# Norm 1 of layer 0 made tile by tile inside the last five vectors of the modulation stage

## The reference, cut to what matters

```python
shift1, scale1, gate1, shift2, scale2, gate2 = jnp.split(mod, 6, axis=-1)   # mod = silu(c) @ w_mod[l] + b_mod[l]
h = rms_norm(x, lp["g_norm1"]) * (1 + scale1) + shift1
u = h @ lp["w_in"]          # the first dense product of the layer; four attention mixers read it
...
x = x + gate1 * mixed
h = rms_norm(x, lp["g_norm2"]) * (1 + scale2) + shift2
x = x + gate2 * expert_choice_ffn(h, ...)
```

## Time and profile before

| | |
|---|---|
| median of 3 runs | 2919.36 us |
| profiled execution, its own time | 2924.13 us |
| its span, first to last instruction | 2922.1 us |
| TensorE busy | 2708.1 us, 93% |
| VectorE, ScalarE, GpSimd busy | 66%, 53%, 16% |
| mean granted clock of TensorE | 0.972 |

### The profile page before, as it was taken

How to read it: one execution, slowest core, us unless ns; L and a number is a source line. 1 busy time by engine, 2 the same in 40 slices (tenths; PEclk the granted TensorE clock), 3 DMA queues, 4 the chain that set the end, 5 groups by cost and what they waited for, 6 DMA issues and landing times.

```text
span 2922.1 us, 40619 instructions
## 1 busy us (share of the span) xinstructions
PE 2708.1 (93%) x13616; PEld 1916.2 (66%) x13616; DVE 1929.7 (66%) x3006; ACT 1555.4 (53%) x2270; POOL 465.5 (16%) x359
## 2 busy tenths in 40 slices
PE   7799999999998999999989999998999699999994
PEld 1387777777773666666658777787777366666662
DVE  7653466435256999999955346653525799999994
ACT  6534443334223877777743444333422387777773
POOL 1030001212211112222113000031122112111111
PEclk9799999999998999999999999999999899999997
DMA  9621111212346999999982111121234599999994
GB/s 362 235 78 42 33 37 49 68 37 68 120 158 223 375 381 376 378 380 378 384 281 77 43 33 37 41 76 37 65 120 151 189 371 385 374 379 380 380 382 165
DMA packets 191183, 593.74 MB, mean 203 GB/s; under 512 B 23628, under 2 KB 33674, under 8 KB 191054
## 3 DMA queue, kind: packets, MB, share of 16 engines
q1 hardware_dynamic: 171646, 527.68, 48.9%
q0 software_dynamic: 19408, 64.37, 7.4%
HBM read 566.73 MB, written 25.23 MB: 203 GB/s over the span
## 4 chain that ended last, share of the span: by engine, by line
PE 79%; DVE 8%; issue 5%; ACT 4%; DMA 3%; SPq 0%; POOL 0%; ACTq 0%; DVEq 0%; POOLq 0%
PE bank L499 22%; PE bank L501 20%; PE bank L500 20%; PE bank L920 4%; PE bank L892 4%; PE bank L910 2%; ACT high L1123 2%; DVE low L1446 2%; DMA ring<-in_w_mod 1%; PE bank L683 1%; DVE st L1692 1%; DVE att L1527 1%; PE bank L1074 1%; PE bank L1035 1%; DVE sigr L1622 1%
## 5 line engine op out<-in xcount | busy, mean ns | idle before, releaser
L1123 ACT ACTIVATE high<-ring 128x1024 fp32r<-128x1024 f32 (+1 forms) x976 | 1023.0, 1052 | 412.3 <-PE bank L501 370.0
L1833 DVE TENSOR_TENSOR low<-ring,high 128x1024 fp32r<-128x1024 f32 x736 | 880.1, 1220 | 73.3 <-ACT high L1123 71.5
L499 PE MATMUL bank<-high,hT_high 128*128 128x512 f32 (+2 forms) x1280 | 521.2, 407 | 25.3 <-ACT sigr L1202 13.6
L500 PE MATMUL bank<-low,hT_high 128*128 128x512 f32 (+2 forms) x1280 | 486.5, 380 | 0.0
L501 PE MATMUL bank<-high,hT_low 128*128 128x512 f32 (+2 forms) x1280 | 484.8, 379 | 0.0
L499 PE MATMUL bank<-high,xeT_high 128*80 128x512 f32 x1056 | 418.8, 397 | 5.8 <-issue 3.5
L501 PE MATMUL bank<-high,xeT_low 128*80 128x512 f32 x1056 | 416.5, 394 | 0.0
L500 PE MATMUL bank<-low,xeT_high 128*80 128x512 f32 x1056 | 416.2, 394 | 0.0
L1446 DVE TENSOR_TENSOR low<-ring,high 128x1024 fp32r<-128x1024 f32 (+2 forms) x240 | 285.5, 1208 | 131.1 <-ACT high L1123 130.0
L1307 ACT ACTIVATE att<-bank,st 128x640 f32<-128x640 f32 (+3 forms) x200 | 136.7, 684 | 348.8 <-DVE st L1697 254.2
L499 PEld LDWEIGHTS bank<-high,hT_high 128*128 128x128 f32 x1280 | 243.9, 191 | 79.1 <-ACT sigr L1202 18.2
(11 more groups left out here) (253 smaller groups left out, 3288.2 us busy)
## 6 DMA issues: line engine op xcount, KB each, us to landing
ring<-in_w_e_gate SPq DMA_DIRECT2D x256, 512.0 KB, 6.2
ring<-in_w_e_up SPq DMA_DIRECT2D x256, 512.0 KB, 7.0
ring<-in_w_e_down SPq DMA_DIRECT2D x256, 512.0 KB, 6.6
ring<-in_w_mod SPq DMA_DIRECT2D x64, 512.0 KB, 6.9
ring<-in_w_gate SPq DMA_DIRECT2D x64, 512.0 KB, 4.6
ring<-in_w_in SPq DMA_DIRECT2D x24, 512.0 KB, 3.8
U<-in_w_mod SPq DMA_DIRECT2D x20, 512.0 KB, 5.0
ring<-in_w_branch SPq DMA_DIRECT2D x16, 512.0 KB, 5.5
```

The source lines that it names most:

```text
L499: nc.tensor.matmul(out, lhs[0], rhs_high, start=start, stop=False)
L500: nc.tensor.matmul(out, lhs[0], rhs_low, start=False, stop=False)
L1123: A(high[:, HSLOT[g], :, 0:w], ring[:, SLOT[g], :, 0:w], ACT.Copy).then_inc(high_done, 1)
L1833: V.tensor_tensor(low[:, SLOT[ahead], :, :], ring[:, SLOT[ahead], :, :], high[:, HSLOT[ahead], :, :].bitcast(F32), ALU.subtract).then_inc( ...
```

## The change

The five tiles of norm 1 of layer 0 are made inside the stage, tile m within vector m+3:

- ScalarE squares tile m behind the first split of vector m+3's step, and writes the high part of the turned tile behind the last split, ahead of `mod_evac`.
- VectorE scales and shifts tile m behind the fifth split of the same step, and writes its low part ahead of the next step's first split.
- TensorE turns tile m behind the last chunk of the vector, into banks 4 to 7. Those banks held the results of `mod_tail`; that result now goes into banks 0 to 3, over the vector's own partial sums.
- `mod_tail(q-1)` stands behind the second chunk of vector q in place of the last, and `mod_copy(q-1)` behind the third split of step q in place of the second split of step q+1. GpSimd loads shift 1 and scale 1 after the store of vector 1, before after that of vector 2.
- TensorE waits for all of norm 1 before the first dense product, whose five tiles then follow with no turns between them. The wait for the last `mod_copy` moves from the end of the stage to the turning of the compressed keys.

Layer 1 is as before.

```diff
+NORM_FROM = N_FIRST - T
+        def norm_bank(q, m, half):
+            return (2 * (m % 2) + half) if q else 4 + 2 * (m % 2) + half
...
@@ TensorE
             def mod_rows(q):
...
                     if k == 0 and q >= 2:
                         pe.wait_ge(mod_row, q - 1)
+                        pe.wait_ge(sum_ready, q - 1)
...
                     ins.then_inc(ring_used, 1)
+                    if k == 1 and q:
+                        mod_tail(q - 1)
+                    if k == KD - 1 and q >= NORM_FROM:
+                        norm_turn(0, q - NORM_FROM)
 
             def mod_tail(q):
...
-                if q >= 2:
-                    pe.wait_ge(sum_ready, q - 1)
                 for h in range(2):
-                    ins = mm(bank(4 + 2 * (q % 2) + h)[0:2, :], pair_sum[:, :], ...
+                    ins = mm(bank(2 * (q % 2) + h)[0:2, :], pair_sum[:, :], ...
...
             for q in range(N_FIRST):
                 mod_rows(q)
-                if q:
-                    mod_tail(q - 1)
             mod_tail(N_FIRST - 1)
-            pe.wait_ge(sum_ready, N_FIRST)
...
-                norm_turn(q1, 0, 0)
+                if l:
+                    norm_turn(q1, 0)
+                else:
+                    pe.wait_ge(norm_low, 2 * T)
                 for m in range(T):
...
-                    if m < T - 1:
-                        norm_turn(q1, m + 1, 0)
+                    if l and m < T - 1:
+                        norm_turn(q1, m + 1)
@@ ScalarE
             for q in range(N_FIRST):
                 for k in range(KD):
                     split_high(KD * q + k + HIGH)
+                    if k == 0 and q >= NORM_FROM:
+                        rms(0, q - NORM_FROM)
+                if q >= NORM_FROM:
+                    norm_highs(0, q - NORM_FROM)
                 mod_evac(q)
@@ VectorE
             for q in range(N_FIRST):
                 for k in range(KD):
+                    if k == 0 and q > NORM_FROM:
+                        norm_lows(0, q - NORM_FROM - 1)
                     split_low(KD * q + k + HIGH)
-                    if k == 1 and q >= 2:
-                        mod_copy(q - 2)
-            mod_copy(N_FIRST - 2)
+                    if k == 2 and q:
+                        mod_copy(q - 1)
+                    if k == 4 and q >= NORM_FROM:
+                        dve.wait_ge(x_in[q - NORM_FROM], 16)
+                        stats(0, q - NORM_FROM)
+            norm_lows(0, T - 1)
             mod_copy(N_FIRST - 1)
@@ GpSimd
-                        if q == 2:
+                        if q == 1:
                             for b in range(2):
                                 pool.wait_ge(mod_out[b], 16)
                             for g in (1, 0):
                                 mod_in(q1, g)
```

More of the change, by code:

```diff
@@ L690, in _, with norm_turn @@
             pe.wait_ge(pair_ready, 2)
+            def norm_turn(q, m):
+                t = T * q + m
+                pe.wait_ge(xn_ready, t + 1)
+                if m >= 2:
+                    pe.wait_ge(norm_low, 2 * (t - 1))
+                for half in range(2):
+                    b = norm_bank(q, m, half)
+                    turn4(lambda k: bank(b, k * P, (k + 1) * P),
+                          lambda k: xn[:, m % 2, (4 * half + k) * P:(4 * half + k + 1) * P], norm_tr)
             def mod_rows(q):
@@ L743, in _ @@
                 q1, q2 = 2 * l, 2 * l + 1
-                def norm_turn(q, m, banks):
-                    t = T * q + m
-                    pe.wait_ge(xn_ready, t + 1)
-                    if m >= 2:
-                        pe.wait_ge(norm_low, 2 * (t - 1))
-                    for half in range(2):
-                        b = banks + 2 * (m % 2) + half
-                        turn4(lambda k: bank(b, k * P, (k + 1) * P),
-                              lambda k: xn[:, m % 2, (4 * half + k) * P:(4 * half + k + 1) * P], norm_tr)
                 if l:
@@ L1142, in mod_evac, with rms, norm_highs @@
                 ins.then_inc(mod_row, 1)
+            def rms(q, m):
+                t = T * q + m
+                if q % 2:
+                    act.wait_ge(x_new, T * (q // 2) + m + 1)
+                else:
+                    act.wait_ge(x_in[m], 16 * (q + 1))
+                if t:
+                    act.wait_ge(sd_ready, t)
+                A(sq, xt_of(q)[:, m, :], ACT.Square, accum_out=ss[:, m:m + 1]).then_inc(sq_done, 1)
+                act.wait_ge(sq_done, t + 1)
+                A(sd[:, m:m + 1], ss[:, m:m + 1], ACT.Sqrt, bias=eps, scale=1.0 / D).then_inc(sd_ready, 1)
+            def norm_highs(q, m):
+                t = T * q + m
+                for half in range(2):
+                    act.wait_ge(norm_tr, 2 * t + half + 1)
+                    high_part(hT[0][:, 4 * half:4 * half + 4, m * P:(m + 1) * P], bank(norm_bank(q, m, half)), norm_high)
+            act.wait_ge(eps_set, 1)
             for g in range(HIGH):
@@ L1158, in later_out_rows @@
                 ins.then_inc(later_ev, 1)
-            act.wait_ge(eps_set, 1)
             for l in range(L):
                 q1, q2 = 2 * l, 2 * l + 1
-                def rms(q, m):
-                    t = T * q + m
-                    if q % 2:
-                        act.wait_ge(x_new, T * l + m + 1)
-                    else:
-                        act.wait_ge(x_in[m], 16 * (q + 1))
-                    if t:
-                        act.wait_ge(sd_ready, t)
-                    A(sq, xt_of(q)[:, m, :], ACT.Square, accum_out=ss[:, m:m + 1]).then_inc(sq_done, 1)
-                    act.wait_ge(sq_done, t + 1)
-                    A(sd[:, m:m + 1], ss[:, m:m + 1], ACT.Sqrt, bias=eps, scale=1.0 / D).then_inc(sd_ready, 1)
-                def norm_highs(q, m):
-                    t = T * q + m
-                    for half in range(2):
-                        act.wait_ge(norm_tr, 2 * t + half + 1)
-                        high_part(hT[0][:, 4 * half:4 * half + 4, m * P:(m + 1) * P], bank(2 * (m % 2) + half), norm_high)
                 def tile_out(pc, m):
@@ L1496, in mod_copy @@
                 ins.then_inc(sum_ready, 1)
-            for g in range(HIGH):
-                split_low(g)
-            for q in range(N_FIRST):
-                for k in range(KD):
-                    split_low(KD * q + k + HIGH)
-                    if k == 1 and q >= 2:
-                        mod_copy(q - 2)
-            mod_copy(N_FIRST - 2)
-            mod_copy(N_FIRST - 1)
             def stats(q, m, last=False):
@@ L1529, in stats, with norm_lows @@
                     V.tensor_tensor(xn[:, m % 2, :], xn[:, m % 2, :], shift_b[q % 2][:, g, :], ALU.add).then_inc(xn_ready, 1)
-            def norm_lows(q, m, banks):
+            def norm_lows(q, m):
                 t = T * q + m
@@ L1535, in norm_lows @@
                     dve.wait_ge(norm_high, 2 * t + half + 1)
-                    low_part(hT[1][:, ks, m * P:(m + 1) * P], bank(banks + 2 * (m % 2) + half), hT[0][:, ks, m * P:(m + 1) * P], norm_low)
+                    low_part(hT[1][:, ks, m * P:(m + 1) * P], bank(norm_bank(q, m, half)), hT[0][:, ks, m * P:(m + 1) * P], norm_low)
+            for g in range(HIGH):
+                split_low(g)
+            for q in range(N_FIRST):
+                for k in range(KD):
+                    if k == 0 and q > NORM_FROM:
+                        norm_lows(0, q - NORM_FROM - 1)
+                    split_low(KD * q + k + HIGH)
+                    if k == 2 and q:
[4 more added lines that the diff above has]
+            norm_lows(0, T - 1)
+            mod_copy(N_FIRST - 1)
             for l in range(L):
                 q1, q2 = 2 * l, 2 * l + 1
-                for m in range(T + 1):
+                for m in range(T + 1 if l else 0):
                     if m < T:
```

21 lines of the change are left out of this document (12 added, 9 removed).

## The result

| | before | after |
|---|---|---|
| median (runs) | 2920.71 us (6; 2918.07 to 2924.93) | 2932.09 us (6; 2929.37 to 2934.82) |
| ratio, with its 95% interval | 1 | 1.0038 [1.0025, 1.0051] |
| profiled execution, span | 2924.13, 2922.1 us | 2932.66, 2930.6 us |
| TensorE, VectorE, ScalarE busy | 2708.1 us, 66%, 53% | 2714.3 us, 66%, 53% |
| mean granted clock | 0.972 | 0.971 |

The change makes the kernel 0.38% slower, 11 us by the medians and 8.5 us between the two spans. The forecast was 2923.6 on a median before of 2919.36, so +4.2 us, with a range of 2913 to 2932. On that footing the ratio gives some 2930, near the upper end of the range: right in its side and short in size. The forecast's likeliest outcome was a change too small to tell (0.49); a measurable loss had 0.36.

A forecast was written before the change was run, and what follows sets the result against it. It saw three engines and the DMA close together inside the stage, then a 32.9 us hole. Stretch +7.0, behind the stage -5.2, dense turns -2.4 and clock +4.8 gave +4.2 us: 2923.6 on the median, range 2913 to 2932.

The forecast's parts named there:

- VectorE becomes the bound, 14.2 us a vector: In the stage, vectors with norm work: VectorE's work rises from 10.4 to 14.2 us, above the 13.6 a vector takes.
- the signs named before the run: Profile after: VectorE steps of 14 to 15 us without idle time from about 70 to 123, vector 6 ending near 110 to 115.
- The walk of the steps: Steps of vectors 3 to 6 followed in order: vector 6 ends at 109.9 against 102.95, stretch +7.0 us.
- The wait for the shift row: Step of vector 3: the shift row is there at 64.8, VectorE is done with L32 by 64.4 and loses 0.5 us.
- Vector 3's own end stays at 62.2 as before.: In the stage: vector 3 ends unmoved at 62.2 us, since the norm instructions follow its last split.
- the list of edits that cost nothing: Four edits at no cost: bank exchange, wait at the compressed keys, DMA bytes, one table load as before.
- the loop that the prediction itself described for the turn: Behind each turn: high parts, evacuation, tail, chunk 3, release of a split; at full clock ends 0.3 us behind VectorE's work.
- The clock, +4.8 us as 3/7 of 11.3: Half clock after TensorE's 2.7 us stops at the ends of vectors 3 to 5: 0 to 11.3 us, taken as +4.8.
- rival 1: The clock falls at every vector's end, so the whole 11.3 counts: +10.7 us, 2930.1; chance 0.27.
- The end, -5.2: Behind the stage: dense product starts 27.7 us behind the end of vector 6 against 32.9, -5.2 us.
- Three turns in the dense product, -2.4: Within the dense product three turns go, 0.8 us each: -2.4 us.
- The table load: ScalarE, first tile's root: one load as before, 1.28 us by the row; any extra falls into the shift row's wait.

The follow-up runs named there:

- the waits filled: Changed kernel with three idle fp32 matmuls of 128x384 ahead of each turn of layer 0: 2923.40 against 2922.05 us, ratio 1.0004.
- short scaling: Changed kernel with layer 0's norm 1 scaling and shifting done on 64 of 1024 columns: 2919.20 against 2922.05 us, ratio 0.9994.
- the six traces: Traces of kernels with the moved tail behind the next vector's second chunk; VectorE reaches chunk 28 between 57.12 and 60.09 us.
- the eight: The other traces, without the tail behind the second chunk; VectorE reaches chunk 28 between 54.27 and 56.18 us.
- the tails alone: Kernel before with only the moved tails and copies, their banks and earlier spread loads; norm 1 behind the stage: 2932.08 against 2922.05 us, ratio 1.0032.
- two mends: Changed kernel with tails behind the fourth chunk and three idle matmuls ahead of each layer 0 turn: 2921.43 against 2922.35 us, ratio 0.9998.

## Why the prediction fell short

- *VectorE becomes the bound, 14.2 us a vector.* Right in the work. With the waits filled, the steps of vectors 5 and 6 are 14.5 us; short scaling gives back 2.6 us a tile, of which 2.0 are VectorE's own. But the signs named before the run were missed: steps of 14 to 15 without idle time, and the end of vector 6 at 110 to 115. The steps took 15.7, 15.9 and 16.8 us with 1.3, 1.6 and 2.45 of waiting, and vector 6 ended at 118.3.
- *The walk of the steps.* Right from chunk 28 on. It put the steps of vectors 4 to 7 at 70.9, 86.6, 101.3 and 116.0; they start at 75.83, 91.58, 107.48 and 124.31. The first two are late by the same 4.9 and 5.0 us, so the step between them is as walked. The wait for the shift row was there, 0.39 us for 0.5:

```profile
69.97 1.28 DVE L1530 SCALAR_TENSOR_TENSOR att<-att,st,M 128x1024 f32<-128x1024 f32 x1 [0.39 <-DMA oTr<-mod_rows]
```

- *"Vector 3's own end stays at 62.2 as before."* **This step failed.** The walk began at chunk 28 from the old trace, and the list of edits that cost nothing had the bank exchange, a wait, the bytes and the table load, but never priced the tails' new place. The 4.9 us that are there already at chunk 28 are in the path; by the averages of the six traces (58.18) and the eight (55.11) 3.1 of them are the place's, and the rest is this execution's. In the changed kernel the same tails two chunks later give 7.7 us back. The sentence claimed a time for instructions that stand behind moved ones on another engine. Its reason, that the norm instructions follow the vector's last split, doesn't hold for ScalarE either: tile 0's squares and root stand behind the first split of the step, VectorE waits 2.37 us behind them (63.69 above), and vector 3's last product ends at 69.5, 7.3 us later than 62.2. The walk itself had VectorE done with chunk 32 only by 64.4, which doesn't go with a vector that ends at 62.2. That part cost no time, since the wait for the shift row follows. What made the place costly is the loop that the prediction itself described for the turn: what stands on TensorE ahead of the third chunk holds up ScalarE's next split.
- *The clock, +4.8 us as 3/7 of 11.3.* The size was near, the working was not. The clock did fall at the end of every vector, as rival 1 had it and as the prediction had named for its own refutation. But it came back sooner: the tails behind it took 1.87 to 2.04 us and not 3.5 (92.75, 109.53 above), so that each event cost less than 4.6. The steps behind vector 4's start lost 1.2 and 2.1 us, 3.3 in all, on top of the walk. So the mechanism was rival 1's, and its price about a third of rival 1's 11.3; that 3/7 of 11.3 comes near it is luck, since it stood for a clock that falls at some of the ends.
- *The end, -5.2.* Right. The first dense matmul stands 26.6 us behind the end of vector 6, for 27.7. The 1.1 us are SyncE's queue and the flight: the first `w_in` chunk came 14.3 behind the end of vector 6 and not 15.6. The chain behind it took 12.3 us for 12.1, and the last tail ended it, as said:

```profile
118.76 0.48 SPq L596 DMA_DIRECT2D qn_b<-in_mla_q_norm  x1
...
128.85 6.82 SPq L554 DMA_DIRECT2D ring<-in_w_in  x8
```

```profile
132.62 0.90 ACT L1132 ACTIVATE high<-ring 128x832 fp32r<-128x832 f32 x1 [1.12 <-DMA ring<-in_w_in]
```

- *Three turns in the dense product, -2.4.* Half right. On TensorE the tiles follow 4.5 us apart, where three of them took 5.4 with a turn behind them, which makes 2.6. The first tile took 7.2 us for 6.0, since the half clock reaches further into it: its matmuls take 0.55 us up to 150.24 and 0.35 behind. Net -1.4.
- *The table load.* ScalarE's timeline of after:

```profile
59.97 1.04 ACT L1162 ACTIVATE att<-att 128x1024 f32<-128x1024 f32 x1
...
61.12 1.28 ACT L1164 ACT_TABLE_LOAD   x1
62.41 0.29 ACT L1164 ACTIVATE st<-st 128x1 f32<-128x1 f32 x1
62.61 4.96 ACT L1132 ACTIVATE high<-ring 128x1024 fp32r<-128x1024 f32 x5
```

From the squares to the next split there are 2.64 us with the load, and 1.37 at the next tile without it, so the load cost 1.27. It stands once in the stage, as forecast, and VectorE idled 2.37 us behind it (63.69 above); the wait for the shift row that was left shows that this was covered. The Trainium skill ("ScalarE: Activation LUTs", What ACT_TABLE_LOAD costs) gives about 2.66 us for a switch of set, the load (about 1.28) and a drain together; this trace shows the load alone.

The sum by the trace: +7.0 for the walk, +4.9 ahead of it, +3.5 left for the clock up to the end of vector 6 (118.3 against 109.9 and 4.9), -6.3, -1.4, together +7.7. The first output behind the dense product's five tiles comes 7.6 us later (173.28 for 165.66). The rest of the 8.5 us of the spans is within what two executions differ by. Without the 4.9 ahead of chunk 28 the measured terms make +2.8, where the forecast had +4.2. That the time still lies at the edge of the range is luck: the range was open upwards for rival 1's 11.3 us of clock, and what filled it was a cost that no term and no rival had. The 7.7 us of the two moved lines are more than 4.9, probably because behind a turn at half clock the tail also stands in the clock's term; no run shows that apart. What stays open is how much of the 10 us of the tails alone is the wait for the bias row: it is in the one trace of that kernel, and the kernel with short scaling has 1.84 us of it, but its load's place was not tried by itself. A second thing was thus missing in the prediction, without a visible effect on the changed kernel's time: the spread loads were moved past a bias row's load, and only the copies' side of that was followed.

## What to carry to other kernels

In a ring that several engines share, ask of every instruction that is moved which product stands behind it on its queue and whom that product releases: ahead of the chunk that gives the next split its slot 1.9 us of small matmuls cost up to 3.6, two chunks later no cost of them could be measured. Start a walk at the first moved instruction of any engine, and not at the first that belongs to the feature. When a stage's bound changes hands, the waits it makes on the next engine cost its clock too; a few idle matmuls in them gave the clock back here, and what two mends give singly is no forecast of what they give together; here 7.7 and 8.7 became 9.8.

## What the runs showed of the hardware

- Three idle matmuls (128x384, 2.1 us) put into waits of 2.5 to 3.1 us went with a granted clock of 1.00 from 82 to 120 us, where it had been 0.91 and 0.83. From 60 to 82 us they made no difference (0.81 and 0.84).
- The tail's four matmuls of five rows take 1.87 us at full clock and 3.57 at half, 0.47 each for 512 columns at full clock. The idle matmuls of 128 rows take 2.10 us for six rows of the trace, 0.35 each for 384 columns. By the column that is the same, so the short contraction is no cheaper.
- An earlier start of the dense product is kept only in part: 4.0 us became 2.8 by the medians, 4.3 became 2.7 by the spans, and 2.9 and 4.4 became nothing where a store came later for it.
